# Reordering the first loads, turns and scalings of a diffusion-transformer block kernel

## What is computed

```python
mod_l = (jax.nn.silu(c) @ w_ada[l] + b_ada[l]).reshape(B, N_MOD, 1, D)
mod_c = (jax.nn.silu(c_ctx) @ w_ada[l] + b_ada[l]).reshape(N_MOD, 1, 1, D)

def _modulate(x, shift, scale):
    return x * (1.0 + scale) + shift

def _swiglu(h, w13, w2):
    a = h @ w13
    return (jax.nn.silu(a[..., :D_FF]) * a[..., D_FF:]) @ w2
```

## Time and profile before

| what | value |
|---|---|
| median of three runs | 2268.97 us |
| the profiled execution, its own time | 2271.54 us |
| its span in the trace | 2269.7 us |
| TensorE matmul busy | 2210.6 us (97%) |
| VectorE busy | 1404.1 us (62%) |
| ScalarE busy | 859.6 us (38%) |
| mean granted TensorE clock, share of 2.4 GHz | 0.987 |
| moved by DMA | 293.08 MB, mean 129 GB/s |

### The profile page before, as it was taken

One profiled execution on the slowest core, in us unless ns is written; L12 is line 12 of the kernel. 1 busy time (PEld: TensorE's weight loads), 2 busy tenths in 40 slices (PEclk: granted clock), 3 DMA queues, 4 the chain that ended last, 5 costly groups with the idle time before them and its releaser, 6 DMA issues.

```text
span 2269.7 us, 31874 instructions
## 1 busy us (share of the span) xinstructions
PE 2210.6 (97%) x11987; PEld 1880.0 (83%) x11991; DVE 1404.1 (62%) x2365; ACT 859.6 (38%) x1477; POOL 158.1 (7%) x169
## 2 busy tenths in 40 slices
PE   9999999999999999999999998989999999999997
PEld 6888888888888888899789977778778888887886
DVE  5676676666446455635562365665777777767787
ACT  3622222222233324532344326651633232326444
POOL 0000000000000000063010003340000000000001
PEclk9999999999999999999999999999999999999999
DMA  7153334454274537323230102322334343438772
GB/s 279 48 157 107 107 117 135 144 163 119 68 270 155 185 107 226 89 93 94 82 103 25 34 5 71 107 85 75 116 104 145 111 147 112 149 117 303 282 232 100
DMA packets 237935, 293.08 MB, mean 129 GB/s; under 512 B 16694, under 2 KB 164846, under 8 KB 237806
## 3 DMA queue, kind: packets, MB, share of 16 engines
q1 hardware_dynamic: 226766, 282.81, 39.3%
q10 hardware_dynamic: 11040, 8.52, 1.2%
HBM read 233.48 MB, written 57.80 MB: 128 GB/s over the span
## 4 chain that ended last, share of the span: by engine, by line
PE 82%; DVE 8%; ACT 4%; DMA 2%; issue 2%; POOL 1%; SPq 0%; DVEq 0%; ACTq 0%; POOLq 0%
PE psum L1272 11%; PE psum L1273 11%; PE psum L1274 11%; PE psum L617 4%; PE psum L618 4%; PE psum L619 4%; PE psum L1439 2%; PE psum L1440 2%; PE psum L1441 2%; PE psum L1910 2%; PE psum L2327 2%; PE psum L1912 2%; PE psum L1911 2%; PE psum L1292 2%; PE psum L1291 2%
## 5 line engine op out<-in xcount | busy, mean ns | idle before, releaser
L1272 PE MATMUL psum<-x_mix_h,x_op_h 128*128 128x512 f32 x640 | 249.9, 390 | 3.2 <-DVE v_sum L1090 3.2
L1273 PE MATMUL psum<-x_mix_l,x_op_h 128*128 128x512 f32 x640 | 249.5, 390 | 0.0
L1274 PE MATMUL psum<-x_mix_h,x_op_l 128*128 128x512 f32 x640 | 249.0, 389 | 0.0
L975 ACT ACTIVATE x_op_h<-raw 128x512 fp32r<-128x512 f32 x140 | 85.9, 627 | 207.4 <-PE psum L1274 126.6
L975 ACT ACTIVATE x_op_h<-w_sum 128x512 fp32r<-128x512 f32 x160 | 97.3, 624 | 158.8 <-DVE w_sum L953 93.7
L1272 PEld LDWEIGHTS psum<-x_mix_h,x_op_h 128*128 128x128 f32 x640 | 120.3, 188 | 28.1 <-DVE x_op_l L981 1.9
L1274 PEld LDWEIGHTS psum<-x_mix_h,x_op_l 128*128 128x128 f32 x640 | 120.2, 188 | 25.2
L1273 PEld LDWEIGHTS psum<-x_mix_l,x_op_h 128*128 128x128 f32 x640 | 120.3, 188 | 23.3
L1439 PE MATMUL psum<-s_high 128*128 128x512 f32 x308 | 121.2, 394 | 3.5 <-DVE s_low L1426 3.4
L1440 PE MATMUL psum<-s_low,s_high 128*128 128x512 f32 x308 | 120.5, 391 | 0.0
L1441 PE MATMUL psum<-s_high,s_low 128*128 128x512 f32 x308 | 120.3, 391 | 0.0
(11 more groups left out here) (410 smaller groups left out, 5710.2 us busy)
## 6 DMA issues: line engine op xcount, KB each, us to landing
raw<-in_ffn_w SPq DMA_DIRECT2D x154, 512.0 KB, 5.1
ada_slice<-in_w_ada SPq DMA_DIRECT2D x56, 512.0 KB, 3.7
f_terms<-g_half SPq DMA_DIRECT2D x77, 256.0 KB, 2.1
s_raw<-f_terms SPq DMA_DIRECT2D x77, 256.0 KB, 3.3
s_raw<-in_ffn_w SPq DMA_DIRECT2D x77, 256.0 KB, 4.1
f_rows<-g_out SPq DMA_DIRECT2D x44, 256.0 KB, 2.0
p_raw<-in_w_in SPq DMA_DIRECT2D x22, 512.0 KB, 5.3
early<-in_w_ada SPq DMA_DIRECT2D x16, 512.0 KB, 6.5
```

The source lines that it names most:

```text
L975: nc.scalar.activation(op_tiles(F, op)[0][:], OP_SOURCE[op], ACT.Copy).then_inc(F.hi, 1)
L1272: nc.tensor.matmul(o, wh[:, k], high(k), start=i < 4 and k == 0, stop=False, skip_group_check=i > 3)
L1273: nc.tensor.matmul(o, wh[:, k], low(k), start=False, stop=False, skip_group_check=i > 3)
L1274: last = nc.tensor.matmul(o, wl[:, k], high(k), start=False, stop=k == KH - 1, skip_group_check=i > 3)
```

## The change

The loads are issued in another order: all 16 modulation pieces, with the first two weight pieces behind the eighth, and only then the x tiles, all eight. The first four parts of the x rows are turned behind both scale sums, the other four between the products of item 0. There is no copy out of PSUM any more: ScalarE makes the high part straight from the turned bank, VectorE makes the full value from the same bank with its own multiply-add and then subtracts. The splitting of the first weights moves on VectorE behind all sums, and on ScalarE ahead of the x rows. The numbers of warm-ups are new, and they go into another bank.

```diff
@@ -305,7 +305,6 @@
 
 
         T1_BANKS = ((3, 4, 5, 6), (4, 5, 6), (4, 5, 6))
-        first_quarter = sem("first_quarter")
         T2_BANKS = ((2, 3), (2, 3, 0, 1), (0, 1, 2, 3))
         T3_BANKS = ((0, 1, 2, 3), (4, 5, 6, 7))
 
@@ -502,16 +501,14 @@
             sp.dma_start(rows_a[0:72, :], b_ada.rearrange("l (r p) -> (l r) p", p=P)).then_inc(bias_in, 16)
             sp.dma_start(rows_a[72:96, :], ln_g.rearrange("l s (r p) -> (l s r) p", p=P)).then_inc(bias_in, 16)
             sp.dma_start(rows_a[96:120, :], ln_b.rearrange("l s (r p) -> (l s r) p", p=P)).then_inc(bias_in, 16)
-            for i in range(4, 6):
+            for i in range(4, KD):
+                early_load(sp, i)
+            for i in range(2):
+                w13_piece(sp, F1, i, 0)
+            for i in range(KD, EARLY):
                 early_load(sp, i)
             for t in range(4):
                 sp.dma_start(y[:, t, :], token_rows(t)).then_inc(x_in[0], 16)
-            for i in range(6, 10):
-                early_load(sp, i)
-            for i in range(2):
-                w13_piece(sp, F1, i, 0)
-            for i in range(10, EARLY):
-                early_load(sp, i)
             for t in range(4, TL):
                 sp.dma_start(y[:, t, :], token_rows(t)).then_inc(x_in[1], 16)
             for i in range(2):
@@ -703,23 +700,22 @@
             sums = psum[:, 2, 0:KD] if v else psum[:, 7, 2 * KD:3 * KD]
             nc.vector.tensor_tensor(in_scale[:, v], sums, early_bias[:, 0], ALU.add).then_inc(mod_ready, 1)
 
-        def first_turned_act(act, k):
-
+        def first_high_act(act, k):
+
+            bias, scale = in_shift[:, 0, k:k + 1], in_scale[:, 0, k:k + 1]
             act.wait_ge(T1.turned, k + 1)
-            nc.scalar.activation(X1.quarter[0, k // KH][:, k % KH], psum[:, T1_BANKS[0][k % 4], :], ACT.Copy)\
-                .then_inc(T1.scaled, 1)
-
-        def first_scaled_act(act, k):
+            nc.scalar.activation(X1.part(0, k, 0, BANK), psum[:, T1_BANKS[0][k % 4], :], ACT.Identity, bias=bias, scale=scale)\
+                .then_inc(T1.high, 1)
+
+        def first_low_dve(dve, k):
+
             rows = X1.quarter[0, k // KH][:, k % KH]
-            bias, scale = in_shift[:, 0, k:k + 1], in_scale[:, 0, k:k + 1]
-            nc.scalar.activation(X1.part(0, k, 0, BANK), rows, ACT.Identity, bias=bias, scale=scale).then_inc(T1.high, 1)
-            nc.scalar.activation(rows, rows, ACT.Identity, bias=bias, scale=scale).then_inc(first_quarter, 1)
-
-        def first_low_dve(dve, k):
             dve.wait_ge(T1.high, k + 1)
-            dve.wait_ge(first_quarter, k + 1)
-            nc.vector.tensor_tensor(X1.part(1, k, 0, BANK), X1.quarter[0, k // KH][:, k % KH],
-                                    X1.part(0, k, 0, BANK).bitcast(F32), ALU.subtract).then_inc(T1.low, 1)
+            nc.vector.tensor_scalar(rows, psum[:, T1_BANKS[0][k % 4], :], in_scale[:, 0, k:k + 1], in_shift[:, 0, k:k + 1],
+                                    op0=ALU.mult, op1=ALU.add).then_inc(T1.scaled, 1)
+            dve.wait_ge(T1.scaled, k + 1)
+            nc.vector.tensor_tensor(X1.part(1, k, 0, BANK), rows, X1.part(0, k, 0, BANK).bitcast(F32),
+                                    ALU.subtract).then_inc(T1.low, 1)
 
         MODS_LATE = N_MOD - 2
         VECTORS = [2, 2, 2] + [1] * (MODS_LATE - 3)
@@ -852,29 +848,30 @@
         def idle_pe(pe, count):
 
             for _ in range(count):
-                nc.tensor.matmul(psum[:, 2, :], idle_square[:], idle_rows[:], start=True, stop=True)
+                nc.tensor.matmul(psum[:, 1, :], idle_square[:], idle_rows[:], start=True, stop=True)
 
         def first_pe(pe, rows_wait):
 
-            beside = (10, 4, 12, 3, 4, 17, 6, 4)
+            beside = (10, 4, 3, 3, 17, 3, 2, 2)
             for k in range(KD):
                 idle_pe(pe, beside[k])
                 early_shift_pe(pe, k)
                 if k == 1:
                     pe.wait_ge(bias_in, 3 * 16)
                     nc.tensor.transpose(psum[:, 0, 0:120], rows_a[0:120, :], ident[0:120, 0:120]).then_inc(rows_turned, 1)
-                if k == 2:
-                    idle_pe(pe, 8)
-                    turn_pe(pe, T1, T1_BANKS, rows_wait, 0)
             early_scale_pe(pe, 0)
-            idle_pe(pe, 10)
+            early_scale_pe(pe, 1)
+            idle_pe(pe, 6)
+            for k in range(4):
+                turn_pe(pe, T1, T1_BANKS, rows_wait, (0, k))
+            idle_pe(pe, 4)
             pe.wait_ge(F1.lo, 2)
             for k in range(KD):
                 pe.wait_ge(T1.low, k + 1)
                 for part in range(2):
                     last = plain_step(pe, F1, 0, part, k)
-                if k == 0:
-                    early_scale_pe(pe, 1)
+                if k < 4:
+                    turn_pe(pe, T1, T1_BANKS, rows_wait, (0, k + 4))
             last.then_inc(F1.ab_ready, 1)
             pe.wait_ge(mod_ready, 2)
 
@@ -3343,13 +3340,10 @@
             act.wait_ge(rows_in, 4 * 16)
             nc.scalar.activation(rows_b[0:16, :], rows_b[0:16, :], ACT.Silu).then_inc(c_silu, 1)
 
-            for k in range(KD):
-                first_turned_act(act, k)
             first_high(act, F1)
-            act.wait_ge(T1.scaled, KD)
             act.wait_ge(mod_ready, 1)
             for k in range(KD):
-                first_scaled_act(act, k)
+                first_high_act(act, k)
             second_block_high(act, F1)
             silu(act, F1, 0)
             half_act(act, F1, T1, T1_BANKS, 1, range(KD))
@@ -3407,14 +3401,12 @@
                     dve.wait_ge(rows_kept, 2)
                     nc.vector.tensor_scalar_add(early_bias[:, 0], params[:, KD:2 * KD], 1.0)
                     nc.vector.tensor_copy(early_bias[:, 1], params[:, 0:KD]).then_inc(rows_kept, 1)
-                if k == 4:
-                    first_low(dve, F1)
+            first_low(dve, F1)
             dve.wait_ge(rows_kept, 3)
             early_known_dve(dve, 0)
-            first_low_dve(dve, 0)
-            first_low_dve(dve, 1)
             early_known_dve(dve, 1)
-            for k in range(2, KD):
+            dve.wait_ge(mod_ready, 2)
+            for k in range(KD):
                 first_low_dve(dve, k)
             second_block_low(dve, F1)
             glu(dve, F1, 0)
```

## The result

| | median | lowest to highest | runs |
|---|---|---|---|
| before | 2270.45 us | 2264.31 to 2274.76 | 20 |
| the change | 2276.89 us | 2269.86 to 2284.53 | 20 |

The ratio is 1.003, with a 95% interval from 1.002 to 1.0041: the change costs 6.4 us, which lies just inside the 0.3% (6.8 us) that the prediction called "no change". The interval reaches over that bound. The prediction was 2271.2 with a range to 2277.5. The direction and the range held, the range by 0.6 us; the size did not (2.2 us foreseen, 6.4 measured). Of the 5.7 us between 2271.2 and 2276.89, 1.5 lie in the kernel before, whose median over 20 runs is 2270.45 and not the 2268.97 of three runs. The profiled execution of the change took 2275.58 us, with a span of 2273.8.

A forecast was written before the change was run, and what follows sets the result against it. TensorE's own sequence at its granted clock was taken to bound the start: first product 48.7 against 46.29, block end 61.5 against 59.3, so 2268.97 + 2.2 = 2271.2 us, range 2263.5 to 2277.5.

The forecast's parts named there:

- What bounds the start: Start up to item 0's end: TensorE's sequence alone is the chain; loads are behind it, but not by much.
- (a): Load order: x tiles move last, so the last modulation piece lands at 29.2, 6 us and more earlier.
- (b): VectorE's modulation sums: latent complete at 29.2, the other at 30.4, then the weights' split; no cost, covered by TensorE.
- (c): Scaling of x rows: turned bank to first low part 2.5 us, before 2.3; VectorE's 1.4 per step hidden behind TensorE's 1.82.
- (d): TensorE's order: two clock falls, both scale sums ahead of the turns; first product 48.7 against 46.29, block end 2.2 us later.
- The sum handed on one for one: From item 0's end onward: what is gained or lost there reaches the kernel's end unchanged, here 2.2 us.
- A: Start: the clock holds and loads set the pace; block end 51.4, 7.9 us gained, 2261.1; chance 0.10.
- B: Start: the second clock fall comes, the first does not; 0.7 us gained, 2268.3; chance 0.10.
- C: Start: the 17 warm-ups do not lift the clock, or it falls again at once; 8.2 to 10.1 us later; chance 0.15.
- D: Turns ahead of the products do not help the clock back; block end 64.6, 5.3 us later, 2274.3; chance 0.08.
- E: Loads: weight pieces hold up SP's queue, piece 8 comes 2 to 3 us later, within "no change"; chance 0.05.

The follow-up runs named there:

- experiment 3: Changed kernel with the load order of the kernel before (x tiles ahead of modulation piece 6, weights behind piece 9); 2280.48 us, ratio 1.005.
- experiment 9: Experiment 6 with 6, 6, 6, 17, 6, 6, 6 warm-ups ahead of the last seven shift groups instead of 4, 12, 8, 17, 6, 6, 6; 2268.01 us, ratio 0.9998.
- experiment 10: Experiment 6's edits with warm-ups 10, 6, 6, 17, 6, 17, 6, 6 and the old load order of experiment 3; 2271.45 us, ratio 1.002.
- experiment 8: Changed kernel with the full value made by ScalarE too, a second scaling out of PSUM, instead of VectorE's multiply-add; 2280.84 us (one run).
- experiment 2: Changed kernel with the context rows' scale sum put back inside item 0, behind its first products; 2276.59 us, ratio 1.0037.
- experiment 4: Changed kernel with experiment 1's warm-ups beside the groups, none added between the sums, and the context's scale sum back inside item 0; 2271.12 us, ratio 0.9998.
- experiment 6: Experiment 4 with six more warm-ups ahead of the latent rows' scale sum; 2268.41 us, ratio 1.0003.
- experiment 5: Kernel before without the 8 warm-ups ahead of its 32 turns and the 3 behind them; 2267.79 us (one run).
- experiment 7: Changed kernel without any warm-up behind the second shift group (40 fewer); 2267.92 us, ratio 0.9989.
- experiment 1: Changed kernel with 31 more warm-ups: 25 beside the shift groups, 6 between the two scale sums; 2268.74 us, ratio 0.9999.

## Why the prediction was right or wrong

**What bounds the start: right.** TensorE's own sequence is the chain from 12 to 50 us, without a wait for a load; experiment 3 shows what it looks like when there is one. That the loads' gain would not reach the end was right too, and experiments 9 and 10 show it from the other side: with TensorE faster, the old order makes it wait and costs 4.0 us, with the slow stretch behind the wait 5.9.

**(a), (b) Loads and sums: right up to piece 8, 1.2 us late behind it.** Piece 8 at 20.05 (forecast 20.2), the weights at 17.04 and 18.78 (17.2 and 19.0). Piece 9 landed only at 22.77 (21.5) and piece 15 at 30.4 (29.2). VectorE's sums were complete at 31.6 instead of 30.4. All of this was covered, as said, by TensorE, which took up piece 9 at 25.97.

**(c) The scaling: right within the change.** 0.81 for VectorE's scaling (0.75 taken), 0.78 and 0.69 for the others, and 2.5 us from the end of the first turns (47.28) to the first low part (49.78). Experiment 8 shows no cost of VectorE's part. That it "hides" behind TensorE's 1.82 per part holds only while VectorE is not made to wait inside the block; with the context's sum inside the block (experiments 2, 4, 6, 9 and 10) the rest of the block went at VectorE's pace.

**(d) TensorE's order: the mechanism right, the sum too small.** Both falls came, in the order forecast, with a rise inside the 17 warm-ups. The term that failed is the place of the first fall: "Three warm-ups, group 2 (piece 5), three warm-ups: 15.4", at full clock. The clock fell at 14.1, so that group 2 took 2.39 and the warm-ups behind it 1.30, which is 1.3 us; another 0.3 was there already, as the first of these warm-ups started at 12.65 and not at 12.3. Group 3 ended at 20.2 instead of 18.6. Later terms brought some back and took a little more: group 6 2.47 against 3.2, sums 6.83 against 6.4, and the first product at 49.96 instead of 48.7. The block took 13.0 instead of 12.8. The end at 63.0 is 1.5 us behind the forecast 61.5; over the three profiles the mean is 1.3.

**The sum handed on one for one: not borne out, and not refuted.** The start explains 3.5 of the 6.4 us. The prediction said that what is lost at the end of item 0 "is handed to the end one for one". On the way it is not: the three profiles of the change go from 3.7, 4.3 and 2.3 us late to 7.6, 7.0 and 6.9 at 625, and end 4.1, 6.4 and 2.4 late. What moves them is the low clock of the later parts, as the table shows, and the sum had no term for it. Starts that are no more than 0.5 us late stayed at 0.3 or better at 625, and those 2.1 or more late were 5.3 to 7.7 late there; behind 625 the two kinds mix again (experiment 10 ends at 0.0). A link between the start and the later falls is therefore possible and not shown.

All executions together, with or without a profile, put a price on the missing 3 us. Their mean granted clock is 0.9893 over 72 executions of the kernel before and 0.9844 over 28 of the change, which is some 22 us more of the low clock per execution. The profiles put 16 of these into the start (26.2 on average against 10.2). The other 6 lie behind it and are, as an estimate, up to 3 us of work. So the change has more of the low clock behind the start too, on average over executions; why, and whether one profile of before stands for its start, stays open. The same count fits with the gains of experiments 6 and 9 not reaching the end: their clocks, 0.9903 and 0.9909 against 0.9894 and 0.9895 of their runs of before, are 4.3 and 6.5 us less of the low clock, where their starts alone have 10 less.

**The rivals.** A (clock holds, block end 51.4) did not come, and its number was too low as well: with the clock held on purpose the block ended at 55.9 and 57.3, since the warm-ups that hold it cost their length and VectorE becomes the pace. B did not come. C did not come either: in the change's own profiles the first product was at 48.5 to 50.6, always before the 53.3 at which C decides. Experiment 8 passed that mark with 53.5, yet by an early first fall (11.9) and not by C's mechanism, since its 17 warm-ups did lift the clock. D, the turns, did not come: they took 2.68 us, the clock rose at 48.2 in their midst, and experiment 5 shows that turns hold a full clock. That they lift a low one is likely and not shown alone; in experiment 7 the clock rose at 46.7, behind 16 turns and within the first three products, with no warm-up near. E came in part: SyncE needed 3.13 us for one issue behind the weights, piece 8 landed as forecast, but piece 9 came 1.3 us late, and all behind it as much. That the long issue did this is not shown: in experiment 7, with the same issue of 3.13 us, the slip came only at piece 13. TensorE was later still, so that it cost nothing, as E itself said.

SyncE's queue in the change (start and length of single issues): that of piece 8, and that of piece 13, which waits until piece 9 has landed:

```profile
11.89 3.13 SPq L662 DMA_DIRECT2D early<-in_w_ada  x1
...
22.77 0.33 SPq L662 DMA_DIRECT2D early<-in_w_ada  x1
```

**What removes the loss.** Five versions stand level with the kernel before (0.9989 to 1.0003), four by more warm-ups (1, 4, 6, 9; the last three with the context's sum back in the block as well), one by hardly any (7). The sum's place alone did nothing for the time (2). None beats it beyond its interval; the best, experiment 7, is at 0.9989 with an upper end of 1.0002.

## What to carry to other kernels

Thinned-out warm-up matmuls were the worst choice: they neither held the granted clock nor came free, and dropping them was 9 us faster than thinning them. Dense along the whole stretch of tiny matmuls they held it and brought item 0 up to 3.5 us forward, but by the time they were no better than hardly any. Loads moved ahead gain only what the engine that consumes them can follow: the last modulation piece came 6 us earlier than before the change, and putting the old order back cost some 4 (experiments 3 and 10, the slow stretches aside). Where the clock's falls are the mechanism, take several profiles of a start before believing one: its edges moved by 2 to 4 us between executions of one kernel, and a difference read at one point of two profiles (7.6 us at 625) was another at the end (4.1). The mean granted clock of all executions is the check that costs no profile.

## What was not expected of the hardware

- Turns alone held the full clock: 32 transposes of 128 x 128 in float32 between two groups of two-column matmuls, 1.00 from 15.9 to 25.9 us (experiment 5).
- TensorE was busy for 32.0 of 33.9 us, with two-column and one-column matmuls until 42.0 and with 16 turns behind them, and had the lower clock throughout (experiment 7). Being busy alone did not keep the clock; in this kernel wide matmuls or turns between the small ones did.
- The row of 17 warm-ups lifted the clock each time, 4.2, 6.0 and 4.2 us behind its start in the three profiles of the change (at 24.3, 27.0 and 22.9) and 5.8 us in experiment 8 (at 29.0).
- Experiments 7 and 9 ended item 0 at 59.25 and 55.89 and were 4.8 us apart at 625, and yet both have the same median, 2267.92 and 2268.01, and profiled executions of 2267.60 and 2267.43. The difference goes into the clock behind 625: 35.9 us of low clock in experiment 9 against 24.3 in experiment 7, half of which difference is 5.8 us.
